# Half of a gate projection moved ahead of the last two pairs' values, and one sigmoid ahead of the low-rank activations, in a two-block fp32 transformer kernel

## What is computed

```
h = rms_norm(x)
cols_a, cols_b, gate_a, gate_b = split(h @ w_in)
y_a, v_first = rwkv7_branch(cols_a, ...)     # token shift, mixing, low-rank projections, scan
y_b = dsa_branch(cols_b, ...)                # selective attention: 8 heads, keys chosen by an index
merged = sigmoid(gate_a) * (y_a @ w_branch_a) + sigmoid(gate_b) * (y_b @ w_branch_b)
x = x + merged @ w_out
```

## Time and profile before

| | us |
|---|---|
| median of the runs shown (3 runs) | 2744.1 |
| lowest and highest | 2741.22, 2744.46 |
| the profiled execution, its own time | 2738.89 |
| its span | 2736.9 |
| PE busy | 2628.1 |
| VectorE busy | 1563.8 |
| ScalarE busy | 1117.8 |

### The profile page before, as it was taken

One profiled execution on the slowest core, in us unless ns is written; L12 is line 12 of the kernel. 1 busy time (PEld: TensorE's weight loads), 2 busy tenths in 40 slices (PEclk: granted clock), 3 DMA queues, 4 the chain that ended last, 5 costly groups with the idle time before them and its releaser, 6 DMA issues.

```text
span 2736.9 us, 38996 instructions
## 1 busy us (share of the span) xinstructions
PE 2628.1 (96%) x16908; PEld 2104.0 (77%) x16908; DVE 1563.8 (57%) x1694; ACT 1117.8 (41%) x1350; POOL 149.9 (5%) x121
## 2 busy tenths in 40 slices
PE   9999999999999999998899999999999899999998
PEld 7996687998989787997565779975667688885477
DVE  5456646456464635456874654458746447564377
ACT  4333534334434543434321454343214345353355
POOL 0002000000011100002011000010110000000000
PEclk9999999999999999999999999999999999999999
DMA  6654335657545254554532435545224257577786
GB/s 231 220 200 139 108 139 184 213 196 226 189 154 185 93 185 159 201 179 144 163 106 78 163 143 201 188 160 167 92 65 155 93 195 282 189 249 258 261 294 229
DMA packets 227774, 484.24 MB, mean 177 GB/s; under 512 B 11708, under 2 KB 45116, under 8 KB 227412
## 3 DMA queue, kind: packets, MB, share of 16 engines
q1 hardware_dynamic: 227604, 481.75, 51.2%
HBM read 477.01 MB, written 2.95 MB: 175 GB/s over the span
## 4 chain that ended last, share of the span: by engine, by line
PE 81%; DVE 11%; ACT 3%; DMA 2%; issue 2%; POOL 1%; SPq 0%; DVEq 0%; ACTq 0%; POOLq 0%
PE psum L732 19%; PE psum L432 12%; PE psum L434 11%; PE psum L433 11%; PE psum L435 10%; PE psum L479 5%; DVE weight_ring_low_halves L427 3%; PE psum L3358 2%; PE psum L2468 2%; PE psum L2554 1%; PE psum L619 1%; ACT weight_high_halves L421 1%; POOL small L653 1%; DVE stage_area_halves L610 1%; PE psum L3288 1%
## 5 line engine op out<-in xcount | busy, mean ns | idle before, releaser
L427 DVE TENSOR_TENSOR weight_ring_low_halves<-weight_ring,weight_high_halves 128x2048 fp32r<-128x2048 f32 (+2 forms) x334 | 737.1, 2213 | 493.8 <-ACT weight_high_halves L421 493.4
L421 ACT ACTIVATE weight_high_halves<-weight_ring 128x2048 fp32r<-128x2048 f32 (+2 forms) x347 | 640.1, 1853 | 536.0 <-PE psum L434 236.6
L432 PE MATMUL psum<-weight_high_halves,stage_area_halves 128*128 128x512 f32 (+4 forms) x1542 | 601.2, 390 | 21.5 <-DVE stage_area_halves L610 10.9
L434 PE MATMUL psum<-weight_high_halves,stage_area_halves 128*128 128x512 f32 (+4 forms) x1542 | 589.1, 382 | 0.0
L732 PE MATMUL psum<-stage_area_halves,weight_high_halves 128*128 128x256 f32 x2880 | 510.4, 281 | 0.0
L433 PE MATMUL psum<-weight_ring_low_halves,stage_area_halves 128*128 128x512 f32 (+4 forms) x1322 | 504.9, 382 | 0.0
L732 PEld LDWEIGHTS psum<-stage_area_halves,weight_high_halves 128*128 128x128 f32 x2880 | 441.9, 189 | 1.1
L732 PE MATMUL psum<-stage_area_halves,weight_ring_low_halves 128*128 128x256 f32 x1440 | 405.5, 282 | 0.0
L432 PEld LDWEIGHTS psum<-weight_high_halves,stage_area_halves 128*128 128x128 f32 x1542 | 290.1, 188 | 122.9 <-issue 50.2
L434 PEld LDWEIGHTS psum<-weight_high_halves,stage_area_halves 128*128 128x128 f32 x1542 | 290.0, 188 | 58.5
L435 PE MATMUL psum<-weight_ring,stage_area 128*128 128x512 f32 x704 | 309.5, 598 | 5.1 <-issue 4.1
(11 more groups left out here) (336 smaller groups left out, 2719.4 us busy)
## 6 DMA issues: line engine op xcount, KB each, us to landing
weight_ring<-in_ffn_w_gate SPq DMA_DIRECT2D x44, 1024.0 KB, 5.1
weight_ring<-in_ffn_w_up SPq DMA_DIRECT2D x44, 1024.0 KB, 5.1
weight_ring<-in_ffn_w_down SPq DMA_DIRECT2D x44, 1024.0 KB, 4.8
weight_ring<-in_w_in SPq DMA_DIRECT2D x36, 1024.0 KB, 7.3
weight_ring<-in_moe_wd SPq DMA_DIRECT2D x27, 1024.0 KB, 4.9
weight_ring<-in_moe_wu SPq DMA_DIRECT2D x25, 1024.0 KB, 6.6
weight_ring<-in_moe_wg SPq DMA_DIRECT2D x22, 1024.0 KB, 6.7
weight_ring<-in_mem_w_kv SPq DMA_DIRECT2D x16, 1024.0 KB, 5.1
```

The lines of the kernel that those rows point to most:

```text
L421: act.raw.activation(self.high_half(name), self.in_slot(name), ACT.Copy).then_inc(*act.mark("high_halves", ("high", name)))
L427: v.raw.tensor_tensor(self.low_half(name), self.in_slot(name), self.high_half(name), ALU.subtract).then_inc(*v.mark("low_halves", ("halves ...
L432: pe.raw.matmul(out, a[1], w[0], start=start, stop=False)
L434: return pe.raw.matmul(out, a[0], w[0], start=False, stop=stop)
```

## The change

There are two edits, in both layers of the second block.

The product of gate (0, 1) with row block 1 is divided by contraction. Parts 0 to 3 are issued in the attention's last step but one, after turn(3) and spread(3) and ahead of values(2) and values(3). Parts 4 to 7 are issued after the attention, where the whole product stood. The sum is built up in bank 3 instead of bank 6. The event for the first weight piece comes with part 3, and the event for the bank with part 7.

ScalarE's sigmoid of the kept gate rows is issued ahead of the wait for the mixed low-rank columns, not behind their activations.

```diff
-    def proj_tensor(self, pe, pr, lhsT, bank, ..., rows=range(MT), only=None):
+    def proj_tensor(self, pe, pr, lhsT, bank, ..., rows=range(MT), only=None, ks=None):
...
-            for k in range(kts):
+            for k in range(kts) if ks is None else ks:
                 w = self.weights(pe, (tag, b, k // 4))
                 mm = self.product(...)
...
+            if ks is not None and kts - 1 not in ks:
+                continue
...
 def pairs_tensor(..., tail=None):
...
         if 1 <= p <= n:
             turn(p - 1)
             spread(p - 1)
+        if p == n and tail is not None:
+            tail()
         if p >= 2:
             values(p - 2)
...
     def prepare_scalar(self, act, l):
         net = self.net
+        act.wait_ge(*act.at(("gate_kept", l)))
+        kept = self.gate[1][:, 0, 0:BANK]
+        act.raw.activation(kept, kept, ACT.Sigmoid).then_inc(...)
         act.wait_ge(*act.at(("mixed_low", l)))
         act.raw.activation(..., ACT.Tanh)
         act.raw.activation(..., ACT.Sigmoid).then_inc(...)
-        act.wait_ge(*act.at(("gate_kept", l)))
-        kept = self.gate[1][:, 0, 0:BANK]
-        act.raw.activation(kept, kept, ACT.Sigmoid).then_inc(...)
...
     def gate_bank(self, nb, j, m):
-        return 7 - m if (nb, j) == (0, 1) else m + (2 if (nb, j) == (0, 0) else 6)
+        return (7, 3)[m] if (nb, j) == (0, 1) else m + (2 if (nb, j) == (0, 0) else 6)
...
-            pairs_tensor(net, pe, f"dsa{l}", ..., between=lambda: self.gate_tensor(pe, l, 0, 1, [0]))
-
-            self.gate_tensor(pe, l, 0, 1, [1])
+            pairs_tensor(net, pe, f"dsa{l}", ..., between=lambda: self.gate_tensor(pe, l, 0, 1, [0]),
+                         tail=lambda: self.gate_tensor(pe, l, 0, 1, [1], range(0, 4)))
+
+            self.gate_tensor(pe, l, 0, 1, [1], range(4, KT))
             self.low_rank_tensor(pe, l)
             self.cumulate_tensor(pe, l)
```

More of the change, by code:

```diff
@@ L480, in passes, with proj_tensor @@
                 yield i, k, mm
-    def proj_tensor(self, pe, pr, lhsT, bank, need=(), turn_1=(), rows_first=False, before_last=(), before=(None, ()), rows=range(MT), only=None):
+    def proj_tensor(self, pe, pr, lhsT, bank, need=(), turn_1=(), rows_first=False, before_last=(), before=(None, ()), rows=range(MT), only=None, ks=None):
         tag, kts = pr["tag"], pr["kts"]
@@ L1062, with pairs_tensor @@
 ALL_KEYS, CAUSAL_KEYS = Keys(False), Keys(True)
-def pairs_tensor(net, pe, tag, heads, to, need_q=(), need_v=(), between=None, late=(None, ())):
+def pairs_tensor(net, pe, tag, heads, to, need_q=(), need_v=(), between=None, late=(None, ()), tail=None):
     n = len(heads) // 2
@@ L2297, in prepare_scalar @@
         net = self.net
+        act.wait_ge(*act.at(("gate_kept", l)))
+        kept = self.gate[1][:, 0, 0:BANK]
+        act.raw.activation(kept, kept, ACT.Sigmoid).then_inc(*act.mark("kept_gate_ready", ("gate", l, 0, 1, 0)))
         act.wait_ge(*act.at(("mixed_low", l)))
@@ L2300, in prepare_scalar @@
         act.raw.activation(self.colsA[:, :, 1664:1792], self.colsA[:, :, 1664:1792], ACT.Sigmoid).then_inc(*act.mark("low_rank_activated", ("activated", l)))
-        act.wait_ge(*act.at(("gate_kept", l)))
-        kept = self.gate[1][:, 0, 0:BANK]
-        act.raw.activation(kept, kept, ACT.Sigmoid).then_inc(*act.mark("kept_gate_ready", ("gate", l, 0, 1, 0)))
         net.turn_copy(act, self.low_rank_turn(l))
@@ L2726, in gate_keep, with gate_tensor @@
         act.raw.activation(self.gate[1][:, 0, 0:BANK], net.ps[:, 7, :], ACT.Copy).then_inc(*net.drained(act, 7, (tag, "full", 0, 0), ("gate_kept", l)))
-    def gate_tensor(self, pe, l, nb, j, rows=range(MT)):
+    def gate_tensor(self, pe, l, nb, j, rows=range(MT), ks=None):
         net = self.net
@@ L2731, in gate_tensor @@
         net.proj_tensor(pe, self.layers[l]["gates"][nb, j], lambda k, m: net.xT[:, k, m * P:(m + 1) * P],
-                        lambda b, m: self.gate_bank(nb, j, m), joined, rows=rows)
+                        lambda b, m: self.gate_bank(nb, j, m), joined, rows=rows, ks=ks)
     def gate_scalar(self, act, l, nb, j, rows=range(MT)):
@@ L2862, in tensor @@
             self.gate_tensor(pe, l, 0, 0)
-            pairs_tensor(net, pe, f"dsa{l}", self.dsa_heads(l), self.dsa_pairs, between=lambda: self.gate_tensor(pe, l, 0, 1, [0]))
-            self.gate_tensor(pe, l, 0, 1, [1])
+            pairs_tensor(net, pe, f"dsa{l}", self.dsa_heads(l), self.dsa_pairs, between=lambda: self.gate_tensor(pe, l, 0, 1, [0]),
+                         tail=lambda: self.gate_tensor(pe, l, 0, 1, [1], range(0, 4)))
+            self.gate_tensor(pe, l, 0, 1, [1], range(4, KT))
             self.low_rank_tensor(pe, l)
```

## The result

| | median us | runs | lowest and highest |
|---|---|---|---|
| kernel before | 2742.72 | 15 | 2740.68, 2747.19 |
| changed kernel | 2749.73 | 15 | 2743.99, 2755.53 |

The ratio is 1.0026 with a 95% interval of 1.0018 to 1.0034, that is 7.1 us (4.9 to 9.3). The forecast was 7.1 us. The profiled execution of the changed kernel took 2748.77 us with a span of 2746.7 us. That is 9.8 us over the span of before, so the two traces differ by more than the medians do, and the reading has to say what the 9.8 us are.

A forecast was written before the change was run, and what follows sets the result against it. PE was 96% busy, and behind the attention the chain ran through parameter loads waiting for values(3). Two layers of 3.57 us gave 7.1 us, 2751.2 us on the 2744.1 median; 8 in 10 range 2746 to 2756.5.

The forecast's parts named there:

- Step 1, the price of the parts: PE ahead of values(2): four of eight contraction parts take 3.57 us; the wait for bank 3 costs nothing.
- Step 2, the stall: PE between values(2) and values(3): both start 3.57 us later, the 1.34 us stall stays, 0 us won.
- Step 3, the loads: SyncE's parameter loads wait for values(3): issued 3.57 us later, so L2357 starts 3.57 us later in each layer; contention 0.
- the sign of being wrong: In the changed trace, any stage behind the attention running less than 3.57 us later per layer would count against the forecast.
- Step 4, VectorE: Last pair's output and mixing shift by 3.57 us; the low-rank rows' copy at 1377.7 in layer 0 hides behind the loads.
- Step 5, ScalarE: Kept gate's sigmoid moves into a 3.70 us wait: 0 us, with none to two more table loads, 0 to 2.56 us, hidden.
- Step 6, PE: Behind the attention, layer 0: L2276 runs 1378.1 to 1382.0, prefix sums start at 1385.1; later work follows in order.
- The rival of the clock: New PE idle in both layers also lowers the clock, 1.7 us once or twice: 2752.9 or 2754.6 us; chance 0.20.
- The rival by which the loads do not bind: Loads land before VectorE is through, leaving VectorE's and PE's own order: 2.1 us slower, 2746.2 us; chance 0.12.

The follow-up runs named there:

- Experiments 2 and 3: 2: changed kernel with two or eight parts ahead, +4.7 and +13.2 us; 3: first three loads counted apart, changed kernel +2.2, kernel before -6.9 us.
- experiment 4: Kernel before, with the parameter loads also waiting for the first half of the gate product behind the attention: 15.1 us slower than before.
- the first run: Kernel before, with only ScalarE's sigmoid of the kept gate moved ahead of the wait for the mixed columns: +0.8 us, ratio 1.0003.
- the parts alone: Changed kernel with the sigmoid put back behind the low-rank activations: 8.2 us slower than the kernel before, ratio 1.0030.
- the run with two parts: Changed kernel with two contraction parts ahead of the values instead of four: 4.7 us slower than the kernel before, ratio 1.0017.

## Why the prediction was right, point by point

- **Step 1, the price of the parts.** 3.57 us were forecast from half of 7.13. The loads were issued 3.44 us later. From start to start a part costs 0.86 us; a row's span runs on to the end of its last product, under the start of the next row, so half of the span is a little too much.
- **Step 2, the stall.** It stayed at 1.34 us. Right.
- **Step 3, the loads.** This was the step that carried the sum. The distance from first load to the scaling was 9.63 and 9.55 us against 10.12 and 9.48. The bound of 0.5 us for contention was not needed. Layer 0 even landed 0.49 us sooner, which nothing in the prediction said, so it came only 2.94 us later and not 3.57: read by its letter, the sign of being wrong "a stage behind runs less than 3.57 us later per layer" came up there, and the prefix sums stand 19.68 us behind spread(3), not 20.3. Neither touches the mechanism. Over all traces with the unsplit wait it lies between 9.47 and 11.23 us, so it is a source of scatter by itself. Experiments 2 and 3 show that the wait for the landing is the cause, and experiment 4 that late loads are enough.
- **Step 4, VectorE.** The copy of the transposed rows started at 1377.52 (1377.7 forecast) and was hidden.
- **Step 5, ScalarE.** No cost, shown by the first run. The table load went ahead with the sigmoid, and Tanh needed none: the low end of the bounds.
- **Step 6, PE.** L2280 was forecast for 1378.1 and started at 1378.05. Its end was not as forecast, 1383.6 instead of 1382.0, because of the clock. The idle ahead of the prefix sums was 0.79 us, not 3.
- **The rival of the clock** had its place in layer 0 and "about 2 us twice" in layer 1, and got 0.20 beside a forecast of 0.60 without it. That split was wrong in kind: the clock is not a case that holds or not but one that falls in some places in some executions, of the kernel before too. Its price of 1.7 us was right for layer 0, where it was covered, and too small for layer 1, 3.14 us, because the low-rank products there ran at half rate all through. The 15 runs reach from 2743.99 us at a mean clock of 0.994 to 2755.53 us at 0.989, and their mean is 0.9916.
- **The rival by which the loads do not bind** was worked out at 2.1 us; with the wait split, which makes it true, 2.2 us were measured. That the two agree so closely is in part luck: layer 1 came as worked out (1.49 us in the trace, 1.5 forecast), and layer 0 did not (1.93 and 0.6), because of the clock. From the first load to L2361, which waits for the seventh, this trace shows 9.6 us. The estimate of 6.2 us worked out from the Trainium skill (DMA: Bandwidth & Descriptors, "Anatomy of one DMA") does not hold for these loads, beside the two weight pieces that are issued right behind them.
- **The time.** 6.5 us of path, read in the trace, and 7.1 us measured leave 0.6 us for the clock and all else on average, with an interval of 2.2 us to either side. The mechanism held, but that forecast and measurement agree to the tenth is luck: the parts cost 0.13 us less in each layer than forecast, layer 0 landed sooner, and the clock took something that the forecast had at nothing. The time itself, 2749.73 us, is 1.5 us below the 2751.2 forecast, as the kernel before came out 1.4 us lower than in the three runs first shown.

## What to carry to other kernels

Work that fills a stall must stand inside it. Before moving it, ask what else counts on the instruction that it is moved past, on the load queue above all: here seven small loads waited for the last product of the attention, and what was put ahead of that product came back on the path of both layers, 0.86 us a part. Where several loads share one counter and the first consumer needs only some of them, count those apart: it was the one edit here that made the kernel faster, by 3.3 and 6.9 us in two measurements.

## What the runs showed of the hardware that I had not expected

- TensorE's clock fell to its lower level (0.50 granted, 1.2 GHz) behind single waits of PE of 2.28 and 2.79 us in the changed kernel and of 4.78 and 5.07 us with the late loads. But the length of a wait does not decide it alone. With the parts alone it fell in layer 1 behind waits of 1.34, 1.12 and 0.94 us, and in the kernel before at 2016 behind waits of 0.68 us. And the same wait of 2.7 to 2.8 us, about 13 us into the kernel, was followed by a fall in 12 of the 14 traces and by none in two: behind it the same 12 records took 4.62 us in the kernel before and 3.06 us in the run with two parts, whose granted clock was 1.00 there. So whether a fall comes differs from one execution to the next, and one trace does not tell what a change does to the clock.
- What a fall costs depends on what lies behind it. In the changed kernel it cost layer 0 nothing, as the slowed products lay ahead of a longer wait, and layer 1 3.14 us.
- Seven row vectors of 256 KB, each one row read out for 128 partitions, took 9.6 to 11.2 us from the first issue to the start of the work that waited for the last, and in the kernel before the third landed 4.8 us after its own issue, 5.7 us after the first issue. Two weight pieces of 1024 KB are issued on the same queue right behind them (from 1371.47 us on in layer 0, 0.87 us after the last of the seven); how much of the time is theirs no run separates.
